# Issuing the normalising product of a projection unit two steps later, in a two-layer hybrid attention encoder

## The chip, the cores and the metric

The kernel runs on the 8 cores of one Trainium2 chip. Each core computes one of the 8 sequences of the batch, with the same program and its own data; the cores don't talk to each other. The metric is the device time in microseconds (us) of the slowest core.

## The reference

Two layers, each over 2048 tokens of width 1024 (per core):

```
h = rmsnorm(x)
q,k,v of 8 dilated heads | q,k,v of 8/2 grouped heads | two gates = split(h @ w_in)
q, k = rmsnorm per head (64 wide) of q and of k
branch A: three dilated windows per head, mixed by their softmax denominators
branch B: +-128 tokens, grouped queries, a sink logit per head
x += (sigmoid(ga) * (yA @ W_A) + sigmoid(gb) * (yB @ W_B)) @ W_out
x += SwiGLU(rmsnorm(x));   x += sigmoid(rmsnorm(x) @ W_pg) * (p @ W_pp)
```

What this text is about is the third line: every projected q and k of a head is multiplied by one over the root of its mean square and by a gain.

## The kernel before

The five engines run programs of their own and wait for each other by semaphores. A small recorder (class Sched) takes every operation in the order in which the Python code issues it, appends it to its engine's program, and adds the waits that the data need: a reader waits for the last writer, a writer for the last writer and all readers. So the order of issue in Python is the order on each engine, and an engine whose next instruction waits does nothing behind it. In the profile nearly all instructions therefore have one of two lines, L113 (with a semaphore update) and L116 (without).

All activations lie with the feature on the partition and the token on the free axis, in chunks of 512 tokens (n = 0 to 3). hT is the normalised input of the layer, ring the streamed weights, P (in the buffer YP) the softmax numerators, psb the 8 banks of PSUM, scr four buffers of 128x512.

A projection unit (qk_unit) makes 128 features (two heads) of q or k for one chunk: 8 matmuls of 128x512 into one bank, a Square on ScalarE (sq), and then its end part, fin: one matmul with a block of ones (ps<-sq,cst_b) into a second bank, so that each row holds the sum of squares of its head; on ScalarE the logarithm and the exponential (scr<-ps, scr<-scr); and on VectorE one product, "in PSUM bank times gain times scr" (scalar_tensor_tensor). A q product writes its target in the buffer X directly; a k product writes kst, and two DMAs on SyncE's queue carry the halves on. There are 52 such units a layer, 104 in all. The product is the last reader of the unit's bank. v units (v_unit, 16 matmuls of 256 columns; vb_unit, 32 of 128) have one copy in place of all that. weave puts the end part of a unit behind the fifth matmul (ninth, seventeenth for v) of the next unit.

Eight units a layer run before attention (upfront), the other 44 are woven into it. run_steps goes through the attention steps: 160 for branch A (4 pairs of heads, 40 steps each), then 92 for branch B. In step i it issues

- on TensorE the scores (up to 4 matmuls into one of two banks), on ScalarE their exp into P, and in each odd step on VectorE one multiplication of the last two P by the exponentiated bias (YP<-YP,Ebuf);
- a late operation, if one is due: the logarithm and exponential of the softmax denominators, and six steps after a group's end the two multiplications that finish the rows of yaT (YP<-X,G);
- from the queue of fill work as many matmuls as the step's share in credit allows (Fill.run; a 512-column matmul costs 0.216);
- on TensorE the values product of step i-4 into one of two output banks, and at a group's end its copy or addition into the accumulator on VectorE (X<-ps, X<-ps,X). In the first eight steps of a pair each step is a group of its own.

Woven units take their main bank in rotation from 4, 5, 6 and the sum-of-squares bank is always 7. The unit three places on thus writes the same main bank again, and its first matmul waits for the product. At the start of a pair (pre) the fill queue is drained, and the first scores of the new pair read all four chunks of q and k that were projected during the last pair.

In the code before, fin issues the product at once:

```
S.op("act", ... scr[ri], in_=psb[b2], func=AF.Ln ...)
S.op("act", ... scr[ri], in_=scr[ri], func=AF.Exp, scale=-0.5)
S.op("dve", ... out=out, in0=psb[bk], scalar=gain, in1=scr[ri] ...)
```

Of the kernel before, what the change touches and what calls it, by code (L numbers as in the profile page):

```python
# [185 lines left out]
def build(n_layers=2):  # L186
# [26 lines left out]
    with ExitStack() as stack:  # L213
# [83 lines left out]
        bank_ctr = [0]  # L297

        def bank8():
            b = bank_ctr[0] % 8  # L300
            bank_ctr[0] += 1
            return b

        ctr = {}

        def rot(name, opts):
            i = ctr.get(name, 0)
            ctr[name] = i + 1
            return opts[i % len(opts)]
# [92 lines left out]
        def wdone(key):  # L402
            wissue(slot_of.pop(key))


        class Fill:
# [10 lines left out]
            def run(self, budget):  # L417
                self.credit += budget
                while self.q and self.credit >= self.q[0][0] * 0.5:
                    c, fn = self.q.popleft()  # L420
                    self.credit -= c
                    fn()
                if not self.q:
                    self.credit = 0.0

            def drain(self):
                while self.q:
                    self.q.popleft()[1]()
                self.credit = 0.0
# [13 lines left out]
        def norm_b(l, gcol, n, pair=True):  # L443
            bk = bank8()
            c0 = 4 if pair else 0
            for c in range(c0, NCH):
                S.op("pe", lambda e, c=c: e.matmul(psb[bk][:, :], lhsT=ones_b, rhs=hc(c, n), start=(c == c0), stop=(c == NCH - 1)),
                     reads=[("h", c, n), "cst_b"], writes=[("ps", bk)], inc=(c == NCH - 1))
            ri = rot("scr", range(4))
            S.op("act", lambda e: e.activation(out=scr[ri][:, :], in_=psb[bk][:, :], func=AF.Ln, bias=1024.0 * EPS),  # L450
                 reads=[("ps", bk)], writes=[("scr", ri)])
            S.op("act", lambda e: e.activation(out=scr[ri][:, :], in_=scr[ri][:, :], func=AF.Exp, scale=-0.5),
                 reads=[("scr", ri)], writes=[("scr", ri)])
            for c in range(NCH):
                S.op("dve", lambda e, c=c: e.scalar_tensor_tensor(
                    out=hc(c, n), in0=xc(c, n), scalar=vd[:, l * NVL + gcol + c:l * NVL + gcol + c + 1], in1=scr[ri][:, :],
                    op0=ALU.mult, op1=ALU.mult),
                    reads=[("x", c, n), ("scr", ri)] + VD, writes=[("h", c, n)])


        def qk_unit(l, key, wcol, width, n, gcol, dst, banks, stat, split=None):
# [18 lines left out]
            def fin():  # L480
# [3 lines left out]
                     reads=[("sq", si), "cst_b"], writes=[("ps", b2)])  # L484
                ri = rot("scr", range(4))
                S.op("act", lambda e: e.activation(out=scr[ri][:, :], in_=psb[b2][:, :], func=AF.Ln, bias=64.0 * EPS),
                     reads=[("ps", b2)], writes=[("scr", ri)])
                S.op("act", lambda e: e.activation(out=scr[ri][:, :], in_=scr[ri][:, :], func=AF.Exp, scale=-0.5),
                     reads=[("scr", ri)], writes=[("scr", ri)])
                if split:  # L490
                    ki = rot("kst", range(4))
                    dst_ = [(ALLP, kst[ki][:, :], False, [], [("kst", ki)])]
                else:
                    dst_ = dst
                for rows, out, tr, rk, wk in dst_:
                    i0, i1 = psb[bk][rows, :], scr[ri][rows, :]
                    if tr:
                        i0 = i0.rearrange("p (s r) -> p r s", r=16)
                        i1 = i1.rearrange("p (s r) -> p r s", r=16)
                    S.op("dve", lambda e, i0=i0, i1=i1, out=out, rows=rows: e.scalar_tensor_tensor(  # L500
                        out=out, in0=i0, scalar=vd[rows, l * NVL + gcol:l * NVL + gcol + 1], in1=i1, op0=ALU.mult, op1=ALU.mult),
                        reads=[("ps", bk), ("scr", ri)] + rk + VD, writes=wk)
                if split:
                    outs, wk = split(n)
                    for rows, out in outs:
                        S.dma("sp", lambda e, rows=rows, out=out: e.dma_start(out=out, in_=kst[ki][rows, :]), ("kstc", ki),
                              reads=[("kst", ki)], writes=wk)
            return [(0.216, mm(k)) for k in range(8)], (0.216, fin)
# [124 lines left out]
        def late_flush():  # L633
            while late:
                late.popleft()[1]()
# [3 lines left out]
        def run_steps(steps, fill, look):  # L639
            n = len(steps)  # L640
            slots = {}
            for i in range(n + look):
                if i < n:
# [15 lines left out]
                    if i % 2 == 1:  # L659
# [6 lines left out]
                             reads=[("P", ps - 1), ("P", ps), ("E", st["e"])], writes=[("P", ps - 1), ("P", ps)])  # L666
                    now[0] = i
                    if late and late[0][0] <= i:
                        late.popleft()[1]()
                    fill.run(st["fill"])  # L670
                if i >= look:
# [16 lines left out]
                    if st["last"]:  # L688
                        g["post"](ob_)
            late_flush()  # L690

        def e_rep(h, off, width, rep):
# [201 lines left out]
        def merge_units(l, h, banks, x_half=None):  # L894
            out = []
            for m in range(8):
                for n2 in range(2):
# [3 lines left out]
                    def mm(which, k, m=m, n2=n2, n=n, st=st):  # L901
                        def f():
                            if x_half is not None and which == "Ga" and m < 4:
                                ri = rot("scr", range(4))
                                st["ra"] = ri
# [30 lines left out]
                            if which in ("Ga", "Gb"):  # L936
                                ri = rot("scr", range(4))
                                st["r" + which[1]] = ri
# [60 lines left out]
        def run_all(units):  # L999
            for _, f in units:  # L1000
                f()

        x_v = x_d.rearrange("(c p) t -> p c t", p=128)
# [82 lines left out]
        for l in range(n_layers):  # L1086
# [27 lines left out]
            if l == 0:  # L1114
# [19 lines left out]
                flips(3)  # L1134
                clear_kb(K_GS)
            wdone(("A", l, 0))
            vb0 = l * NVL
# [6 lines left out]
            for part in ("p3", 0, 1, 2, 3):  # L1144
                vt_loads(0, part)
            dbank = lambda: rot("dense", (4, 5, 6))
            sbank = lambda: 7
            kq = [kb_unit(l, n, dbank, sbank) for n in range(NTC)] + [vb_unit(l, t, dbank) for t in range(4)]
# [23 lines left out]
            for c in range(4):  # L1172
# [12 lines left out]
                def pre(c=c):  # L1185
                    fill.drain()
                    fill.add(segs[c])
                ps_[0]["pre"] = pre
# [8 lines left out]
            for n in range(2):  # L1197
                S.alias(R_X(n), K_X01[n])
                load_x(src_x, n, skey(n), (1,))
            mbank = lambda: rot("mbank", (4, 5, 6, 7))  # L1200
            rest = weave([qbu[(cc, n)] for n in (2, 3) for cc in range(4)]) + [(0.0, lambda l=l: wdone(("QB", l)))]
# [11 lines left out]
            def pre_of(b):  # L1213
                if b == 0:
                    fill.add(rest)
                if b == 8:
                    assert ("QB", l) not in slot_of
# [46 lines left out]
            def gu_half(fb, cb, w, mi, fi, half):  # L1264
# [14 lines left out]
                for n in ns:  # L1279
                    ri = rot("scr", range(4))  # L1280
                    bg, bu = bks[(0, n)], bks[(1, n)]
# [57 lines left out]
            def ple(n, ms):  # L1339
                for m2 in ms:  # L1340
# [9 lines left out]
                    for k in range(2):  # L1350
                        S.op("pe", lambda e, k=k, bP=bP, m2=m2: e.matmul(
                            psb[bP][:, :], lhsT=WPP[:, k, m2 * 128:(m2 + 1) * 128], rhs=ppT[:, k, n * TC:(n + 1) * TC], start=(k == 0), stop=(k == 1)),
                            reads=["wpp", "ppT"], writes=[("ps", bP)], inc=(k == 1))
                    ri = rot("scr", range(4))
                    S.op("act", lambda e, bG=bG, ri=ri: e.activation(out=scr[ri][:, :], in_=psb[bG][:, :], func=AF.Sigmoid),
# [113 lines left out]
```

How the kernel before makes its waits and increments, by code:

```python
    def _waits(self, eng, toks, rawkeys):  # L78
        need = {}
        for (k, v) in toks:
            if v > need.get(k, 0):
                need[k] = v
        for k, v in need.items():
            if k == eng and (eng == "pe" or k not in rawkeys):
                continue
            if self.waited[eng].get(k, 0) >= v:
                continue
            self.waited[eng][k] = v
            s = self._sem(k)
            self.prog[eng].append(lambda e, s=s, v=v: e.wait_ge(s, v))
            self.nwait += 1
# [8 lines left out]
    def op(self, eng, fn, reads=(), writes=(), inc=True):  # L100
        toks = self._deps(reads, writes)
        raw = set()
        for r in reads:
            st = self.res.get(r)
            if st and st[0]:
                raw.add(st[0][0])
        self._waits(eng, toks, raw)
        s = self._sem(eng)
        call = _capture(fn)
        if inc:
            self.count[eng] += 1
            tok = (eng, self.count[eng])
            self.prog[eng].append(lambda e, c=call, s=s: getattr(e, c[0])(*c[1], **c[2]).then_inc(s, 1))
        else:
            tok = (eng, self.count[eng] + 1)
            self.prog[eng].append(lambda e, c=call: getattr(e, c[0])(*c[1], **c[2]))
        self._record(tok, reads, writes)
# [1 line left out]
    def dma(self, eng, fn, chan, reads=(), writes=()):  # L119
# [4 lines left out]
        tok = (chan, self.count[chan])  # L124
        call = _capture(fn)
        self.prog[eng].append(lambda e, c=call, s=s: getattr(e, c[0])(*c[1], **c[2]).then_inc(s, 16))
        self._record(tok, reads, writes)
```

## Time and profile before

| | us |
|---|---|
| median of 3 runs | 2242.71 (2242.6 to 2243.81) |
| the profiled execution | 2242.86 |
| its span, slowest core (core 3) | 2241.3 |
| spans of the 8 cores | 2232.8 to 2241.3 |
| TensorE busy on core 3 | 2081.4 (93%) |
| VectorE busy | 1126.8 (50%) |
| ScalarE busy | 947.0 (42%) |

The span is the time from a core's first instruction to its last; the device time of the same execution is 1.6 us more. Shares over the whole span mix stages. Attention with its woven projections takes about 84 to 332 us and 1188 to 1436 us of the span (up to the end of the last woven projection); in these stretches ScalarE and VectorE are far busier than on average. Matmuls are pipelined: one of 512 columns is shown with 0.38 us but follows the one before it after 0.21 us. "Granted clock" is the TensorE clock that the chip let through, as a share of full speed; 1.00 is 2.4 GHz, 0.50 is 1.2 GHz, and a stretch between them holds some of each.

### The profile page before, as it was taken

Reading aid. Unit: us, or ns where it says so; the run is one execution under the profiler, and the core shown is the slowest. Engines: PE = TensorE matmul, PEld = TensorE weight load, DVE = VectorE, ACT = ScalarE, POOL = GpSimd, SP = SyncE. Lnnn points to the kernel's source line nnn. Section 1 sums busy time; section 2 is a strip of 40 time slices with the busy share of each in tenths; the row PEclk is TensorE's granted clock in tenths of the full one; section 3 lists DMA queues with packets and bytes.
Section 4 is the critical chain, followed back from the end, with each engine's and each line's share of the span. In section 5 each row is a group of like instructions: output and inputs, shape, how many; then the busy total and the mean of one; then the engine's idle time right before and its main releaser. Section 6 shows DMA issues by size and latency. Waiting matters only on the chain.

```text
span 2241.3 us, 32719 instructions; the slowest of 8 cores (2232.8 to 2241.3 us)
## 1 busy us (share of the span) xinstructions
PE 2081.4 (93%) x11296; PEld 1023.9 (46%) x11296; DVE 1126.8 (50%) x1647; ACT 947.0 (42%) x1527; POOL 186.7 (8%) x201
## 2 busy tenths in 40 slices
PE   5888879899999999999989887898999999999998
PEld 1555534344444444444446564343444444444443
DVE  3677877555421221125855787765654112211376
ACT  4688886544311001113656888854523110011232
POOL 4110000000110000000130100000000100010000
PEclk9999999999999999999999999999999999999999
DMA  8752432474644203531253524253535721062113
GB/s 230 134 69 48 74 57 45 69 132 57 94 57 62 38 1 47 71 39 29 83 127 86 67 56 80 32 94 57 113 49 83 96 34 26 1 89 29 30 34 135
DMA packets 240187, 154.43 MB, mean 69 GB/s; under 512 B 88795, under 2 KB 217979, under 8 KB 239995
## 3 DMA queue, kind: packets, MB, share of 16 engines
q0 software_dynamic: 152240, 85.01, 29.1%
q1 hardware_dynamic: 87788, 67.33, 10.3%
q8 instruction: 96, 1.57, 0.3%
q14 instruction: 63, 0.52, 0.1%
HBM read 211.07 MB, written 21.00 MB: 104 GB/s over the span
## 4 chain that ended last, share of the span: by engine, by line
PE 83%; ACT 7%; issue 4%; DVE 4%; DMA 2%; ACTq 0%; DVEq 0%; POOL 0%; SPq 0%; POOLq 0%
PE ps L116 67%; PE ps L113 15%; ACT YP L113 2%; DVE X L113 2%; ACT G L113 2%; ACT scr L113 2%; DMA ring<-w_in 1%; DVE YP L113 1%; DVE hT L113 1%; ACT sq L113 1%; ACT hT L113 0%; ACT L113 0%; DMA X<-kst 0%; DVE scr L113 0%; ACTq L90 0%
## 5 line engine op out<-in xcount | busy, mean ns | idle before, releaser
L116 PE MATMUL ps<-hT,ring 128*128 128x512 bf16 x4536 | 1116.9, 382 | 13.6 <-DMA ring<-w_in 8.1
L116 PEld LDWEIGHTS ps<-hT,ring 128*128 128x128 bf16 x4536 | 443.1, 99 | 509.1 <-issue 28.3
L113 ACT ACTIVATE scr<-ps 128x512 f32<-128x512 f32 x480 | 274.7, 596 | 894.4 <-PE ps L113 871.7
L113 ACT ACTIVATE YP<-ps 128x512 bf16<-128x512 f32 x504 | 291.6, 592 | 158.5 <-PE ps L113 148.9
L113 DVE TENSOR_TENSOR G<-ps,scr 128x512 bf16<-128x512 f32 x176 | 113.4, 686 | 465.3 <-PE ps L113 465.3
L116 PE MATMUL ps<-G,YP 128*128 128x512 bf16 x1280 | 297.2, 379 | 0.0
L113 DVE TENSOR_TENSOR X<-ps,X 128x512 f32<-128x512 f32 x192 | 131.1, 688 | 177.8 <-PE ps L113 177.6
L113 PE MATMUL ps<-hT,ring 128*128 128x512 bf16 x648 | 218.2, 381 | 0.1
L113 DVE TENSOR_TENSOR YP<-YP,Ebuf 128x1024 bf16<-128x1024 bf16 x252 | 173.1, 688 | 84.3 <-ACT YP L113 83.3
L116 PEld LDWEIGHTS ps<-G,YP 128*128 128x128 bf16 x1280 | 125.3, 98 | 151.0
L113 PE MATMUL ps<-YP,G 128*128 128x512 bf16 (+2 forms) x536 | 159.5, 301 | 6.3 <-DVE X L113 3.5
L113 DVE SCALAR_TENSOR_TENSOR hT<-X,vd,scr 128x512 bf16<-128x512 f32 x192 | 129.3, 746 | 60.7 <-ACT scr L113 60.7
L116 PE MATMUL ps<-YP,G 128*128 128x128 bf16 (+2 forms) x864 | 126.0, 243 | 34.3 <-DVE X L113 28.4
L113 DVE SCALAR_TENSOR_TENSOR scr<-scr,ps 128x512 f32<-128x512 f32 x128 | 86.4, 686 | 95.9 <-PE ps L113 91.9
L113 ACT ACTIVATE hT<-X 128x2048 bf16<-128x2048 f32 x48 | 89.9, 1901 | 91.7 <-DVE X L113 88.8
L116 PE MATMUL ps<-X 128*128 128x128 bf16 (+1 forms) x768 | 102.7, 230 | 23.8 <-ACT YP L113 17.5
L116 PEld LDWEIGHTS ps<-YP,G 128*128 128x128 bf16 x864 | 72.1, 99 | 104.9 <-issue 57.2
L116 PE MATMUL ps<-G,ring 128*128 128x512 bf16 x448 | 109.4, 379 | 6.7 <-DVE X L113 6.7
L126 POOL DMA_DIRECT2D ring<-w_in x66 | 58.1, 889 | 614.8 <-PE ps L113 558.1
L113 PE MATMUL ps<-X,G 128*128 128x512 bf16 x216 | 83.2, 385 | 16.3 <-ACT YP L113 15.7
L113 PEld LDWEIGHTS ps<-hT,ring 128*128 128x128 bf16 x648 | 63.8, 98 | 72.3 <-issue 2.1
L113 ACT ACT_TABLE_LOAD x46 | 59.0, 1283 | 84.7 <-PE ps L113 78.6
(82 smaller groups left out, 1813.6 us busy)
## 6 DMA issues: line engine op xcount, KB each, us to landing
ring<-w_in POOLq DMA_DIRECT2D x42, 512.0 KB, 8.1
X<-x SPq DMA_DIRECT2D x16, 1024.0 KB, 13.8
YP<-w_ffn_down POOLq DMA_DIRECT2D x8, 1408.0 KB, 18.5
ring<-w_ffn_gate POOLq DMA_DIRECT2D x20, 512.0 KB, 6.2
ring<-w_ffn_up POOLq DMA_DIRECT2D x20, 512.0 KB, 7.9
ring<-w_out POOLq DMA_DIRECT2D x8, 1024.0 KB, 9.6
xscr<-X SPq DMA_DIRECT2D x8, 1024.0 KB, 4.2
X<-xscr SPq DMA_DIRECT2D x8, 1024.0 KB, 8.6
```

Source lines behind the costliest of these rows:

```text
L113: self.prog[eng].append(lambda e, c=call, s=s: getattr(e, c[0])(*c[1], **c[2]).then_inc(s, 1))
L116: self.prog[eng].append(lambda e, c=call: getattr(e, c[0])(*c[1], **c[2]))
L126: self.prog[eng].append(lambda e, c=call, s=s: getattr(e, c[0])(*c[1], **c[2]).then_inc(s, 16))
```

## The change

The product, and the DMAs behind it, go into a function tail that is not called at once but held. A counter called clock is advanced by 0.44 at each attention step and by the listed cost of each piece of fill work (0.216 for a matmul of 512 columns). A held tail is issued when the counter has gone on by 2.6 since its fin. In branch A a step with its fill adds between 0.9 and 1.2 to the counter, so that 2.6 is two to three steps. Whoever takes a bank or a scr buffer that a held tail still reads (claim) has it and all older ones issued first, and all are issued at the start of a pair, at the end of a run of steps, before block 0 and block 8 of branch B, and after upfront.

```diff
+        clock = [0.0]
+        held = collections.deque()
+        def hold(delay, bank, si, fn):
+            held.append((clock[0] + delay, bank, si, fn))
+        def tick(c):
+            clock[0] += c
+            while held and held[0][0] <= clock[0]:
+                held.popleft()[3]()
+        def claim(bank=None, si=None):
+            while any((bank is not None and h[1] == bank) or (si is not None and h[2] == si) for h in held):
+                held.popleft()[3]()
+        def held_flush():
+            while held:
+                held.popleft()[3]()
...
@@ Fill.run, Fill.drain, run_all: after each piece of work
                     fn()
+                    tick(c)
...
@@ qk_unit, fin
-                ri = rot("scr", range(4))
+                ri = next_scr()
...
-                for rows, out, tr, rk, wk in dst_:
-                    ... product on VectorE ...
-                if split: ... two DMAs on SyncE's queue ...
+                def tail():
+                    for rows, out, tr, rk, wk in dst_:
+                        ... product on VectorE ...
+                    if split: ... two DMAs on SyncE's queue ...
+                hold(2.6, bk, ri, tail)
...
@@ run_steps
                     now[0] = i
+                    tick(0.44)
                     if late and late[0][0] <= i:
                         late.popleft()[1]()
...
             late_flush()
+            held_flush()
...
@@ start of a pair
                 def pre(c=c):
                     fill.drain()
+                    held_flush()
```

No operation is added or removed.

## Rows read from the trace of the kernel before

**Rows 1.** Spans and mean granted TensorE clock, fastest and slowest core.
```profile
core 1: 2232.8 us, clock 0.990
core 3: 2241.3 us, clock 0.985
```

**Rows 2.** Busy time by stretch, layer 0, branch A then start of B: stretch, length, engines, PEclk, DMA.
```profile
84.00:292.00 208.00, 176.57 (x1651) 121.34 (x1649) 157.77 (x219) 169.99 (x312) 15.92 (x16) 0.96 0.40 70
292.00:332.00 40.00, 31.69 (x138) 13.01 (x139) 28.07 (x41) 34.39 (x63) 3.97 (x6) 0.96 0.42 76
```

**Rows 3.** Waits, 84 to 332 us: who for whom, us in total, times, longest.
```profile
ACT YP L113 <- PE ps L113: 25.3, 41, 2.2
DVE X L113 <- ACT scr L113: 17.5, 16, 2.5
PE ps L116 <- DVE X L113: 14.2, 13, 3.5
DVE kst L113 <- ACT scr L113: 11.5, 10, 3.1
```

**Rows 4.** Timeline, pair 0: start, length, engine, operation, [idle before, releaser].
```profile
118.34 1.07 ACT L113 ACTIVATE YP<-ps 128x512 bf16<-128x512 f32 x2
118.35 0.81 PE L116 MATMUL ps<-hT,ring 128*128 128x512 bf16 x3
118.54 1.10 DVE L113 SCALAR_TENSOR_TENSOR X<-ps,vd,scr 128x512 bf16<-128x512 f32 x1 [0.93 <-ACT scr L113]
119.55 0.69 DVE L113 TENSOR_TENSOR YP<-YP,Ebuf 128x1024 bf16<-128x1024 bf16 x1
120.09 0.27 PE L116 MATMUL ps<-ring,hT 128*128 128x256 bf16 x1
120.15 2.42 DVE L113 TENSOR_TENSOR YP<-X,G 64x512 bf16<-64x512 f32 x2
120.44 0.58 ACT L113 ACTIVATE sq<-ps 128x512 bf16<-128x512 f32 x1
```

**Rows 5.** Timeline, the same pattern in pair 1, and its last case in layer 1.
```profile
172.21 2.40 DVE L113 TENSOR_TENSOR YP<-X,G 64x512 bf16<-64x512 f32 x2
172.34 0.59 PE L116 MATMUL ps<-hT,ring 128*128 128x512 bf16 x2
...
1329.85 2.39 DVE L113 TENSOR_TENSOR YP<-X,G 64x512 bf16<-64x512 f32 x2
1329.92 0.39 PE L116 MATMUL ps<-ring,hT 128*128 128x128 bf16 x4
```

**Rows 6.** Timeline, starts of pair 2 and pair 3.
```profile
189.50 0.53 PE L116 MATMUL ps<-X 128*128 128x128 bf16 x3
190.41 0.69 DVE L113 TENSOR_TENSOR YP<-YP,Ebuf 128x1024 bf16<-128x1024 bf16 x1 [0.84 <-ACT YP L113]
...
239.78 0.38 PE L116 MATMUL ps<-X 128*128 128x128 bf16 x3 [0.16 <-ACT YP L113]
...
241.41 0.69 DVE L113 TENSOR_TENSOR YP<-YP,Ebuf 128x1024 bf16<-128x1024 bf16 x1 [0.25 <-ACT YP L113]
```

**Rows 7.** Timeline, branch B.
```profile
320.25 1.47 DVE L113 TENSOR_TENSOR X<-X,G 64x512 bf16<-64x512 f32 x2
320.49 0.59 PE L116 MATMUL ps<-hT,ring 128*128 128x512 bf16 x2
```

**Rows 8.** Timeline, a place without late multiplications.
```profile
114.09 0.68 DVE L113 TENSOR_TENSOR YP<-YP,Ebuf 128x1024 bf16<-128x1024 bf16 x1
114.19 0.27 PE L116 MATMUL ps<-ring,hT 128*128 128x256 bf16 x1
```

**Rows 9.** Timeline, start of pair 1.
```profile
146.45 0.75 DVE L113 SCALAR_TENSOR_TENSOR kst<-ps,vd,scr 128x512 bf16<-128x512 f32 x1 [1.28 <-ACT scr L113]
147.95 0.33 PE L116 MATMUL ps<-YP,G 128*128 128x128 bf16 x3 [1.45 <-DVE X L113]
```

**Rows 10.** Busy time by stretch behind that wait, columns as in Rows 2.
```profile
152.00:156.00 4.00, 3.59 (x20) 1.90 (x21) 3.09 (x6) 1.20 (x2) 0.00 (x0) 0.68 0.14 35
```

More of the change, by code:

```diff
@@ L301, in bank8, with next_scr @@
             bank_ctr[0] += 1
+            claim(bank=b)
             return b
+        def next_scr():
+            ri = rot("scr", range(4))
+            claim(si=ri)
+            return ri
         ctr = {}
@@ L427, in drain @@
                 while self.q:
-                    self.q.popleft()[1]()
+                    c, fn = self.q.popleft()
+                    fn()
+                    tick(c)
                 self.credit = 0.0
@@ L484, in fin @@
                      reads=[("sq", si), "cst_b"], writes=[("ps", b2)])
-                ri = rot("scr", range(4))
+                ri = next_scr()
                 S.op("act", lambda e: e.activation(out=scr[ri][:, :], in_=psb[b2][:, :], func=AF.Ln, bias=64.0 * EPS),
@@ L489, in fin @@
                      reads=[("scr", ri)], writes=[("scr", ri)])
[L490 to L494, printed above, removed]
-                for rows, out, tr, rk, wk in dst_:
[L496 to L507, printed above, removed]
+                def tail():
+                    if split:
+                        ki = rot("kst", range(4))
+                        dst_ = [(ALLP, kst[ki][:, :], False, [], [("kst", ki)])]
+                    else:
+                        dst_ = dst
+                    for rows, out, tr, rk, wk in dst_:
+                        i0, i1 = psb[bk][rows, :], scr[ri][rows, :]
+                        if tr:
+                            i0 = i0.rearrange("p (s r) -> p r s", r=16)
+                            i1 = i1.rearrange("p (s r) -> p r s", r=16)
+                        S.op("dve", lambda e, i0=i0, i1=i1, out=out, rows=rows: e.scalar_tensor_tensor(
+                            out=out, in0=i0, scalar=vd[rows, l * NVL + gcol:l * NVL + gcol + 1], in1=i1, op0=ALU.mult, op1=ALU.mult),
+                            reads=[("ps", bk), ("scr", ri)] + rk + VD, writes=wk)
+                    if split:
+                        outs, wk = split(n)
+                        for rows, out in outs:
+                            S.dma("sp", lambda e, rows=rows, out=out: e.dma_start(out=out, in_=kst[ki][rows, :]), ("kstc", ki),
+                                  reads=[("kst", ki)], writes=wk)
@@ L903, in f @@
                             if x_half is not None and which == "Ga" and m < 4:
-                                ri = rot("scr", range(4))
+                                ri = next_scr()
                                 st["ra"] = ri
@@ L936, in f @@
                             if which in ("Ga", "Gb"):
-                                ri = rot("scr", range(4))
+                                ri = next_scr()
                                 st["r" + which[1]] = ri
@@ L999, in run_all @@
         def run_all(units):
-            for _, f in units:
+            for c, f in units:
                 f()
+                tick(c)
         x_v = x_d.rearrange("(c p) t -> p c t", p=128)
@@ L1145, in build, with dbank, sbank @@
                 vt_loads(0, part)
-            dbank = lambda: rot("dense", (4, 5, 6))
-            sbank = lambda: 7
+            def dbank():
+                b = rot("dense", (4, 5, 6))
+                claim(bank=b)
+                return b
+            def sbank():
+                claim(bank=7)
+                return 7
             kq = [kb_unit(l, n, dbank, sbank) for n in range(NTC)] + [vb_unit(l, t, dbank) for t in range(4)]
@@ L1186, in pre @@
                     fill.drain()
+                    held_flush()
                     fill.add(segs[c])
@@ L1199, in build, with mbank @@
                 load_x(src_x, n, skey(n), (1,))
-            mbank = lambda: rot("mbank", (4, 5, 6, 7))
+            def mbank():
+                b = rot("mbank", (4, 5, 6, 7))
+                claim(bank=b)
+                return b
             rest = weave([qbu[(cc, n)] for n in (2, 3) for cc in range(4)]) + [(0.0, lambda l=l: wdone(("QB", l)))]
@@ L1215, in pre_of @@
                     fill.add(rest)
+                if b in (0, 8):
+                    held_flush()
                 if b == 8:
@@ L1279, in gu_half @@
                 for n in ns:
-                    ri = rot("scr", range(4))
+                    ri = next_scr()
                     bg, bu = bks[(0, n)], bks[(1, n)]
@@ L1353, in ple @@
                             reads=["wpp", "ppT"], writes=[("ps", bP)], inc=(k == 1))
-                    ri = rot("scr", range(4))
+                    ri = next_scr()
                     S.op("act", lambda e, bG=bG, ri=ri: e.activation(out=scr[ri][:, :], in_=psb[bG][:, :], func=AF.Sigmoid),
```

## The prediction

> **What bounds the kernel now.** I read the page first. TensorE is busy for 93% of the span, but that is an average; the change touches only the units woven into attention, so the stretches that count are about 84 to 332 us and the same stretch of layer 1, 1188 to 1436. There I read the busy time by stretch, then the waits, and then the timeline of TensorE, VectorE and ScalarE around single products, beside the order in which the code issues them.
>
> The stretches show three engines that are all nearly full and none that is full: of 208 us TensorE 177, ScalarE 170, VectorE 158, and at the start of branch B ScalarE 34.4 of 40 [rows 2]. Such a stage is bound by its chain: scores, exp, multiplication by the bias, values product, and two score banks that let TensorE run only two steps ahead of the exps. The waits say what the change aims at: VectorE stands 17.5 + 11.5 = 29.0 us in layer 0 in front of a product that waits for the exponential (scr) of its unit, in 26 places, while TensorE waits 14.2 us for VectorE's output X [rows 3]. If the first caused the second, it would pay to move the products.
>
> The timeline says that mostly it doesn't. Take the product at 118.54, for which VectorE waits 0.93 us; the bias multiplication behind it starts at 119.55. But this one needs two exps that ScalarE runs from 118.34 to 119.41, *behind* the unit's own exponential, since ScalarE too works in order [rows 4]. Without the product it would start at 119.5 at best. The wait in front of a product is a hole that ScalarE's order leaves in VectorE's time, and the product sits in that hole. Taken out of it, it is done later, and nothing else is done much earlier.
>
> **What the change does, part by part.** 104 products and the DMAs of those that go by kst are issued later, with the same lengths. So the question is only who waits for them, and who waited behind them. I placed each in the order of issue by adding up 0.44 a step and the costs of the fill work, which is arithmetic on the code, and looked up which rows stand before and behind that place.
>
> *Bank reuse behind late multiplications (cost).* In the case above the counter has gone on by 2.6 when TensorE is in the group of three matmuls at 118.35. By then VectorE's program holds, ahead of the product, the bias multiplication and the two multiplications YP<-X,G of 2.42 us together. VectorE comes to the product after 119.5 + 0.6 + 2.4 = about 122.1 (I give it half a microsecond for starting without the product) and ends it 1.1 us later, at 123.2. TensorE wants the bank, for the first matmul of the unit three places on, at 120.09 [rows 4]: a stall of 3.1 us where there was none. In pair 1 the same order ends the two multiplications at 174.6, the product at 175.6 or slightly before, and the bank is wanted at 172.34: 3.2 us; the pattern's last case is at 1329.85 and 1329.92, where the end is 1332.2 + 1.1 less 0.6: 2.8 us [rows 5]. There are three a layer. 2 x (3.1 + 3.2 + 2.8) = 18.2 us. The product's own place is what the code says, so this is the surest term; bounds 14 and 20.
>
> *Start of a pair (cost).* The last q product of pairs 1 and 2 comes due in the last step before the new pair, behind that step's bias multiplication, and the new pair's first scores read it. TensorE is there at 189.50; the bias multiplication runs at 190.41 to 191.10, so the product ends at 192.1: 2.6 us. Into pair 3 TensorE is there at 239.78, the bias multiplication at 241.41 and the product ends at 243.1, less 0.7 because what stood behind the old product moves up: again 2.6 us [rows 6]. Four in two layers, 10.4 us, bounds 7 and 12. Into pair 1 the product is done in time, since the fill work of pair 0 ends earlier.
>
> *Branch B (cost).* One place a layer has two multiplications of 1.47 us together ahead of the product, which then ends at 321.7 + 0.6 = 322.3, against a bank wanted at 320.49 [rows 7]: 1.8 us, 3.6 in all. The last units of B are not delayed, as gate units claim their banks at once.
>
> *Small shifts (cost).* At some 22 other places the product slips by one or two short VectorE instructions. In the one with the largest shortfall the bias multiplication ends at 114.8 and the product of 1.1 us would end at 115.9, less some 0.6 for starting earlier, against a bank wanted at 114.19: 1.1 us by this reckoning [rows 8]. The others lie between nothing and that, and a TensorE that has just stood still for one bank is less far ahead at the next. Bounds 0 and 22 x 1.1 = 24 us; I take 0.3 each, 6.6 us, nearer the low end since the long stalls come among them.
>
> *Copies that move up (gain).* In the first eight steps of a pair each step ends with a copy that frees an output bank, and there a ready copy does stand behind a waiting product. VectorE waits 1.28 us for the product at 146.45, the copy comes behind it, and TensorE stands for 1.45 us until 147.95 [rows 9]. There are four places like it, one at the start of each of pairs 1 and 2 in both layers; at the mean wait in front of a kst product, 11.5 / 10 = 1.15 us [rows 3], that is 4.6 us gained, bounds 0 and twice that, 9.2, if the product's own length leaves the path too.
>
> *Elsewhere.* The eight units before attention have idle VectorE time around them and banks that are wanted microseconds later, so they cost nothing; the work that hides them is the v unit behind, and without it at most the 0.7 us of a copy, once a layer. In SyncE's queue the kst DMAs now stand behind at most two loads that were issued before; nobody needs their data before the next pair. Waits are neither added nor harder to meet.
>
> New stalls sum to 18.2 + 10.4 + 3.6 + 6.6 = 38.8 us. Not all of it lengthens the span, since ScalarE still has work while TensorE stands. In the first case ScalarE's work that was released before the stall ends at 121.02 [rows 4]. TensorE comes back at 123.2 and its next scores end about half a microsecond later, so ScalarE idles 2.6 us, of which 0.6 were idle before: 2.0 of 3.1 us. I take 0.6 of all, 23.3 us, bounds 0.4 and 0.8 (16 and 31). Less the gain of 4.6: +18.7 us on the profiled execution's 2242.86 (a span of 2241.3 and 1.6 around it), which is 2261.6. That execution is 0.15 us above the median of the runs, so 2261.4 for the median.
>
> By one rule of the Trainium skill the sum would be zero. Its page "Perfetto Trace Analysis", section "Identifying Performance Opportunities", has one improve the most-contended engine, the one with the highest occupancy, and look for what opens the gaps on it. VectorE is the least occupied of the three here [rows 2], so by that rule gaps moved about on it would change nothing, and the time would be 2242.9. The trace does not bear that out for this change, since its slack is at single banks and not in the mean.
>
> **The rivals.**
>
> *More low clock.* TensorE ran at its lower level, 1.2 GHz, for part of 152 to 156 us, behind the stalls at the start of pair 1 (0.68 granted over 4 us) [rows 10]. That is 0.32 x 4 x 2 = 2.6 us at half speed and 1.3 us of work lost, at least, since the stretch may go on. There are twelve new stalls of 1.8 to 3.2 us; if each brings one that is 16 us, if half of them do 8 us, for 2270 or more. For it: the slowest core has the lowest clock, and is 8.5 us behind the fastest [rows 1]. Against: cores of the same program differ in this, and the stalls that go away take some low stretches with them.
>
> The page "TensorE: Matmul & The Clock Gate", section "Part 1: The HAM clock gate", states that the lower clock is the default and that activity lifts it; by that rule new stalls can only add such stretches, which is this rival's time of 2270. The rows fit it where a low stretch follows a stall.
>
> *Absorbed.* ScalarE is the real limit, TensorE uses up the new stalls where it would have waited for exps anyway (ScalarE waited for TensorE for 25.3 us in 41 places [rows 3], so there is room both ways), and the small gain cancels the rest: 2244, within 2240 and 2247. Against it: in pair 0 the score matmuls hardly wait.
>
> *Faster.* The waits in front of the products are on the path after all. VectorE's multiplications and copies move up by what it waited, 29.0 us a layer [rows 3]; TensorE's stalls for VectorE's X, 14.2 us in layer 0 [rows 3] and about as much in layer 1, shrink by a third, 9.5 us, and no bank is wanted before its product. Its place is the first eight steps of a pair and its price 2242.9 - 9.5 = 2233. It decides if the new stalls for banks and first scores stay under some 7 us over both layers, that is, if VectorE runs ahead of my reckoning by the 2 us by which the products are late. I find it unlikely because of the multiplications YP<-X,G.
>
> That the change does nothing, because claims force the products out at once, can be excluded: by the sum of costs only 3 of 104 are issued by a claim.
>
> **How the numbers follow.** The sum as worked out (2251 to 2269): 0.48. With more low clock (2269 and above): 0.20. Absorbed: 0.17. Faster: 0.15. The predicted time is that of the first, 2261.4. The range takes it whole, reaches over most of the low-clock case to 2278, and down over part of the absorbed one to 2240; outside lie most of the faster case and a small part of the upper one. A change under 0.2% (4.5 us) can't be told from none here. Faster by more than that: 0.15; within: 0.17; slower: 0.48 + 0.20 = 0.68.
>
> **What would show it.** In the waits: VectorE's waits for ScalarE's scr nearly gone, from 29.0 us; in their place VectorE waits for the exps (ACT YP). TensorE's waits for VectorE's X up from 14.2 to 35 us or so in layer 0, with single ones near 3 us at a matmul ps<-hT,ring or ps<-ring,hT about 36 us after branch A's start, and one of 2 to 3 us at the first scores (ps<-X) of pairs 2 and 3. The wait of 1.45 us at the start of pair 1 shrinks below 0.5. The prediction is wrong if TensorE's waits for X grow by less than 7 us over both layers, or if they grow as said and the span does not: then the share of 0.6 was the error.

## The result, and the profile after

The change makes the kernel slower: two runs of 2310.76 and 2316.38 us against 2242.6 to 2243.8, a ratio of 1.0314, interval 1.0284 to 1.0345. Forecast were 2261.4, and 2278 as the upper end; the direction was right, the size was not. The profiled execution is the one of 2310.76. In some executions, the profiled ones of `e5_flush_before_pair` and `e12_half_repaired` among them, some cores ran at a lower clock than the rest; the times given below leave such executions out, the intervals of these two runs still hold some, and in these two I read core 3.

Spans and granted clock, fastest and slowest core of the changed kernel, against [rows 1]:

```profile
core 0: 2301.8 us, clock 0.978
core 7: 2309.2 us, clock 0.974
```

All eight cores are slower by about as much, and the clock is lower on each. Next comes the busy time by stretch of nearly the same work as in [rows 2]. Matmul for matmul, 332 us of the kernel before is 364.8 us here; the second window stops at 360, so that the two rows hold 12 matmuls fewer:

```profile
84.00:315.00 231.00, 182.35 (x1645) 124.35 (x1644) 156.05 (x216) 169.99 (x309) 15.15 (x16) 0.93 0.37 62
315.00:360.00 45.00, 30.67 (x132) 11.92 (x129) 29.10 (x42) 35.02 (x65) 3.97 (x6) 0.91 0.38 60
```

VectorE and ScalarE do the same work in the same busy time; TensorE is busy for 6 us more in the first stretch, at a clock of 0.93 instead of 0.96, and the rest is standing still. The waits of 84 to 360 us, against [rows 3]:

```profile
DVE YP L113 <- ACT YP L113: 80.5, 61, 4.5
ACT YP L113 <- PE ps L113: 47.9, 53, 3.0
PE ps L116 <- DVE X L113: 36.0, 19, 3.5
```

and, of the kernel before, 84 to 332 us:

```profile
DVE YP L113 <- ACT YP L113: 24.8, 32, 1.9
```

VectorE's waits for scr are gone, as the change intends. Its waits for the exps (ACT YP) grew by 55.7 us, by more than the 29.0 that went, as the exps themselves now wait longer for TensorE. TensorE's waits for VectorE's X went from 14.2 to 36.0 us, and to 40.1 if the window goes on to 365 us and so takes in the stall at 360.14; the forecast was "to 35". ScalarE now waits 47.9 us for TensorE instead of 25.3. Even the engine that was to be the limit starves.

Timeline of the first case of [rows 4] in the changed kernel:

```profile
120.01 0.69 DVE L113 TENSOR_TENSOR YP<-YP,Ebuf 128x1024 bf16<-128x1024 bf16 x1 [1.61 <-ACT YP L113]
120.62 2.37 DVE L113 TENSOR_TENSOR YP<-X,G 64x512 bf16<-64x512 f32 x2
123.03 1.06 DVE L113 SCALAR_TENSOR_TENSOR X<-ps,vd,scr 128x512 bf16<-128x512 f32 x1
124.24 0.27 PE L116 MATMUL ps<-ring,hT 128*128 128x256 bf16 x1 [2.57 <-DVE X L113]
```

The bias multiplication doesn't start earlier; it waits 1.61 us for exps where the product used to stand. The product comes behind 2.37 us of late multiplications, and TensorE starts 0.15 us after its end, having stood for 2.57 us. Two more places, the first scores of pair 2 and a gate unit of branch B:

```profile
201.11 1.06 DVE L113 SCALAR_TENSOR_TENSOR X<-ps,vd,scr 128x512 bf16<-128x512 f32 x1
202.42 0.52 PE L116 MATMUL ps<-X 128*128 128x128 bf16 x3 [3.02 <-DVE X L113]
...
357.14 0.69 DVE L113 TENSOR_TENSOR YP<-YP,Ebuf 128x1024 bf16<-128x1024 bf16 x1 [4.50 <-ACT YP L113]
357.75 1.47 DVE L113 TENSOR_TENSOR X<-X,G 64x512 bf16<-64x512 f32 x2
359.25 0.75 DVE L113 SCALAR_TENSOR_TENSOR X<-ps,vd,scr 128x512 bf16<-128x512 f32 x1
360.14 1.44 PE L116 MATMUL ps<-hT,ring 128*128 128x512 bf16 x3 [4.16 <-DVE X L113]
```

Since the order of TensorE's instructions is the same in both kernels, each matmul can be set beside itself. Three sums over both attention stretches come of that, and they carry the rest of this text:

- **single stalls**: what TensorE newly stands at the reader or the bank of a product, place by place: 65.3 us (38 banks with 48.8, six first scores with 16.5);
- **net stalls**: all of TensorE's stalls over 0.15 us, after minus before: +44.9 us, since other stalls shrink beside the new ones;
- **low clock**: the time at 1.2 GHz (0.50 granted), after minus before: +50.5 us.

The attention stretches are 66.4 us longer. The remainder, 66.4 - 44.9 = 21.5 us, I put down to matmuls running slower: 0.43 us for each us of low clock. That is a difference and not a measurement of its own; it also holds what changed in stalls under 0.15 us.

### The profile page after: what moved, and what is told of

Its sections match the earlier page's. It is cut to its first block, busy times and chain, and to the rows that moved or that the text cites. A ratio compares the mean times of both kernels' runs of the same rounds, so it can differ in the third digit from the quotient of the medians.

```text
span 2309.2 us, 32550 instructions; the slowest of 8 cores (2301.8 to 2309.2 us)
## 1 busy us (share of the span) xinstructions
PE 2104.4 (91%) x11296; PEld 1032.8 (45%) x11296; DVE 1127.3 (49%) x1647; ACT 951.2 (41%) x1527; POOL 186.6 (8%) x201
## 4 chain that ended last, share of the span: by engine, by line
PE 80%; ACT 7%; DVE 6%; issue 5%; DMA 2%; DVEq 0%; ACTq 0%; POOL 0%; SPq 0%; POOLq 0%
PE ps L116 66%; PE ps L113 15%; DVE X L113 3%; ACT YP L113 3%; DVE YP L113 2%; ACT G L113 2%; DMA ring<-w_in 1%; ACT scr L113 1%; DVE hT L113 1%; ACT sq L113 1%; ACT hT L113 0%; ACT L113 0%; DVE kst L113 0%; DMA X<-kst 0%; DVEq L90 0%
## 5 line engine op out<-in xcount | busy, mean ns | idle before, releaser
L116 PE MATMUL ps<-hT,ring 128*128 128x512 bf16 x4536 | 1128.5, 385 | 41.9 <-DVE X L113 26.9
L116 PEld LDWEIGHTS ps<-hT,ring 128*128 128x128 bf16 x4536 | 444.0, 99 | 549.2 <-issue 73.2
L116 PE MATMUL ps<-G,YP 128*128 128x512 bf16 x1280 | 297.2, 379 | 0.0
L116 PEld LDWEIGHTS ps<-G,YP 128*128 128x128 bf16 x1280 | 125.2, 98 | 151.0
L116 PE MATMUL ps<-YP,G 128*128 128x128 bf16 (+2 forms) x864 | 128.1, 246 | 23.9 <-DVE X L113 21.0
L116 PE MATMUL ps<-X 128*128 128x128 bf16 (+1 forms) x768 | 105.2, 235 | 36.6 <-DVE X L113 14.6
L116 PEld LDWEIGHTS ps<-YP,G 128*128 128x128 bf16 x864 | 75.2, 100 | 92.6 <-issue 44.6
L116 PE MATMUL ps<-G,ring 128*128 128x512 bf16 x448 | 109.7, 380 | 6.7 <-DVE X L113 6.7
L116 PE MATMUL ps<-ring,hT 128*128 128x256 bf16 (+1 forms) x728 | 89.9, 260 | 20.8 <-DVE X L113 17.5
```

The source lines that it names most:

```text
L116: self.prog[eng].append(lambda e, c=call: getattr(e, c[0])(*c[1], **c[2]))
```

## The experiments

My theory: the loss is TensorE standing at banks and first scores whose product is late, and the low clock that comes with it. The rivals: VectorE's new order or the later DMAs cost by themselves; ScalarE is the limit; the low clock has another reason.

**1. The late product without its bank** (`e1_late_no_bank`), and **2. the same on the kernel before** (`e2_early_no_bank`).

```diff
-  i0, i1 = psb[bk][rows, :], scr[ri][rows, :]
+  i0, i1 = scr[ri][rows, :], scr[ri][rows, :]
```

> The changed kernel, but the late product reads scr twice in place of its PSUM bank and scr, so that no bank is held by it (this leaves the projected value out of q and k). Order and number of instructions are those of the changed kernel; the product may be some tenths shorter. My theory: the added time is made by banks that come free late (some 49 us of single stalls at matmuls of the projection units, of which what the rest gives back is about 15) and the low clock behind them. Without them only the stalls at first scores of pairs (14.6 us) and part of the low clock are left: 2252 to 2265. Rival A, that VectorE's order itself, or late DMAs of k, costs the time: 2290 or more. Rival B, low clock that comes for another reason than stalls: 2260 to 2275 with a granted clock that stays below 0.980.

> The kernel before with the same edit (the product reads scr twice, not its bank), which leaves the projected value out of q and k. It tells what the bank costs when the product is early, and is the base for the run above. My theory: little, since most banks come free before they are wanted: 2236 to 2243. Rival: even the early products hold TensorE up, then 2225 or less.

Measured: 2262.3 to 2263.9 for the first (1.0089, 1.0073 to 1.0106), 2240.2 for the second (one run), 3 us under the kernel before. So holding the bank costs 2310.8 - 2263 = 48 us of the 68, or 45 if the 3 us are taken off, with the order on VectorE and the DMAs unchanged. Rival A (2290 or more) is out. Rival B is not: 2262 to 2264 us lies in its range as well as in that of my theory, five of the eight cores show a granted clock below 0.980, and beside only 15.2 us of single stalls there are 29.9 us more of low clock. Of the rest, 13.2 + 2.0 us are the six first scores, read in the timeline of core 5 of the first run. TensorE's waits for X over the whole span in this run, and then in the changed kernel (37.8 us in 30 places in the kernel before):

```profile
PE ps L116 <- DVE X L113: 43.0, 23, 3.5
```

```profile
PE ps L116 <- DVE X L113: 86.6, 44, 5.4
```

**3. Products ahead of the late multiplications** (`e4_ahead_of_late`), and **4. all of them issued four steps before a pair ends** (`e5_flush_before_pair`).

```diff
# 3, run_steps
-  late.popleft()[1]()
+  fn_ = late.popleft()[1]
+  if fn_ in heavy: held_flush()     # heavy: the operations YP<-X,G and X<-X,G
+  fn_()
# 4, each pair
+  ps_[36]["pre"] = held_flush
```

> The changed kernel, but held products are issued ahead of a late multiplication of branch A (YP<-X,G) or branch B (X<-X,G) whenever one comes due; all others stay two steps late. My theory: the stalls of 2.6 to 3.2 us at six banks and of 2.0 at two go (17.1 + 4.0 = 21 us), with the low clock that follows them (some 0.4 us for each us of stall): 2310.8 - 21 to 29 = 2282 to 2290. Rival, that only 0.6 of such stalls lengthens the span: 2298. Rival, that ScalarE sets the time: no change, 2308 or more.

> The changed kernel, but held products are issued at step 36 of each pair (four steps before its end), so that a product which the next pair's first scores read is late by less. My theory: the six stalls of 1.9 to 3.3 us at first scores (16.5 us) shrink to the 0.5 us of before or so: 2310.8 - 14 to 20 = 2291 to 2297. Rival, that these stalls are shared with ScalarE's work and cost only part: 2302 or more. If products that become due after step 36 are still late, the stalls stay and so does the time.

Measured: 2284.9 to 2285.4 for 3 (1.0189, 1.0168 to 1.0209), as expected; 2295.1 and 2295.6 for 4 (1.0271, 1.0212 to 1.033), as expected. The bank of the first case comes free 0.18 us late in place of 2.57, the first scores of pair 3 wait 0.39 us in place of 3.33. Both classes of stalls are real, and both cost more than their length: 25 us for 21 us of single stalls, 15.5 for 13.

**5. Nothing held in branch B** (`e6_no_hold_in_b`): `hold` is replaced by a direct call of the product there.

> The changed kernel, but the eight units woven into branch B issue their product at once, as before; in branch A all are held. My theory: the stalls at the banks of these units and of the gate units behind them go, in the changed kernel 0.49 + 2.00 + 4.16 + 1.53 us in layer 0 and 0.49 + 0.32 + 2.00 + (5.43 - 1.63) us in layer 1, 14.8 us in all, and the low clock behind them: by the ratios of the two runs before (25 us gained for 21 us of stalls, 15.5 for 11.3) that is 15 to 20 us, 2291 to 2296. Rival, that my claim in the prediction (gate units are not delayed) was right and these stalls belong to something else: 4 us, 2307.

Measured: 2298.7 to 2299.7 (1.0247, 1.0232 to 1.0262), 12 us less than the changed kernel. The 14.8 us of single stalls are gone, so the rival (4 us) is out, but the gain is under the 15 to 20 that I expected: where the product no longer holds TensorE up, the Square of the last unit does, as before. From core 3 of this run, and from the changed kernel, where that wait had shrunk:

```profile
351.90 0.38 PE L113 MATMUL ps<-sq,cst_b 128*128 128x512 bf16 x1 [3.00 <-ACT sq L113]
```

```profile
354.69 0.44 PE L113 MATMUL ps<-sq,cst_b 128*128 128x512 bf16 x1 [2.03 <-ACT sq L113]
```

**6. The three repairs together** (`e9_repaired`: 3, 4 and 5).

> The changed kernel with the three repairs together: held products ahead of late multiplications, all issued at step 36 of a pair, none held in branch B. My theory: what is left are the small shifts of branch A, by the single stalls of the two runs before about 20 us at banks and 3 to 5 us at first scores, and they cost their own length: 2243 + 24 = 2267, within 2260 and 2272. Rival, that the wait in front of early products is worth something, which shows once the large stalls are gone: 2250 or less. Rival, that the repairs add up without any rest: 2243.

Measured: 2258.2 to 2260.0 (1.0067, 1.0053 to 1.0082), 2 us below the range of my theory. 22.8 us of single stalls are left, none over 1.3 us, and the kernel is 16 us above the one before. This is the part of the loss that no repair at the large places reaches: products that slip by one or two short VectorE operations at 31 banks and four first scores. The first case of [rows 4] here:

```profile
122.11 1.08 DVE L113 SCALAR_TENSOR_TENSOR X<-ps,vd,scr 128x512 bf16<-128x512 f32 x1
123.10 2.42 DVE L113 TENSOR_TENSOR YP<-X,G 64x512 bf16<-64x512 f32 x2
123.33 0.27 PE L116 MATMUL ps<-ring,hT 128*128 128x256 bf16 x1 [0.18 <-DVE X L113]
```

**7. Half the delay** (`e7_delay_half`: `hold(1.3, ...)`), and **8. half the delay with the repairs** (`e12_half_repaired`).

> The changed kernel with a hold of 1.3 on the counter in place of 2.6, that is one to two steps. My theory, that each product costs what it is later than its bank or reader is wanted: about half of the products no longer pass the late multiplications and are one bias multiplication (0.69 us) less late, so that the single stalls fall from 63 to some 25 to 35 us and the time to 2265 to 2280. Rival, that the delay as such costs (products behind any bias multiplication): 2295 or more. Rival, that a short hold already takes the products out of VectorE's way at no cost: 2243 or less.

> The changed kernel with the short hold of 1.3 and the three repairs (ahead of late multiplications, issued at step 36 of a pair, none held in branch B). In the run with the short hold alone 10.3 us of single stalls were left and it took 2257.8, that is 14 us above the kernel before; four of them, 2 x 2.93 at the banks behind YP<-X,G and 2.5 + 0.5 in branch B, are what the repairs aim at. My theory: a late product costs by its stalls and the low clock behind them alone, so without them nothing is left of the loss, and the gain from copies that move up stays: 2238 to 2245. Rival, that moving products costs by itself: 2250 or more. Rival, that the waits in front of the products were on the path: 2233 or less, as the run in which no product waits.

Measured: 2257.1 to 2259.8 for 7 (1.006, 1.0047 to 1.0074), below the range that I had given, because far fewer banks come late than I thought: 10.3 us of single stalls are left, most of it in three (2.93 at the bank behind YP<-X,G in each layer, 2.5 at the last gate bank). Run 8 takes these away, 3.0 us remain, and the time is 2244.9 to 2247.1 beside 2243.6 to 2248.9 for the kernel before on that chip (0.9968, 0.9923 to 1.0013: no difference), at the upper end of my theory's 2238 to 2245 and above it. So in time, moving a product costs nothing where its bank isn't wanted; it also brings nothing. On core 3 of run 7 attention is 11.6 us longer, of which 5.1 are net stalls and the other 6.5 go with 20.3 us more of low clock. The stretch around the stall of 2.93 us in run 7, core 3:

```profile
120.00:124.00 4.00, 1.13 (x12) 0.52 (x9) 3.86 (x5) 1.87 (x4) 0.00 (x0) 1.00 0.02 4
124.00:128.00 4.00, 3.94 (x24) 2.87 (x25) 1.72 (x3) 1.17 (x2) 0.00 (x0) 0.57 0.26 64
128.00:132.00 4.00, 4.00 (x41) 2.94 (x40) 2.52 (x4) 3.82 (x8) 0.00 (x0) 1.00 0.15 35
```

TensorE stands, and right behind the stall the granted clock is 0.57 over 4 us, that is 3.4 us at 0.50, then 1.00 again. In the kernel before the same work ran at 1.00.

**9. What the change could gain at best** (`e3_early_no_wait`): the early product takes the normaliser of the unit before.

```diff
+  rj = (ri - 1) % 4
-  i0, i1 = psb[bk][rows, :], scr[ri][rows, :]
+  i0, i1 = psb[bk][rows, :], scr[rj][rows, :]
```

> The kernel before, but the product multiplies by the normaliser of the unit before (which is long there) in place of its own, so that VectorE never waits for the logarithm and exponential. The product stands at its early place (q and k are scaled by another token chunk's or head's normaliser). This is what the change could gain at best. My theory: the waits of 29 us a layer in front of products lie beside ScalarE's work; free of them only the copies and banks behind them move up: 2233 to 2241. Rival, that these waits are on the path: 2225 or less.

Measured: 2232.1 to 2242.4 (0.9963, 0.9949 to 0.9977), three of the five within 2232.1 and 2233.2: 8 to 10 us, at the lower edge of my range. Of the 58 us that VectorE waited in front of products in both layers, most comes back; VectorE waits for the exps in their place, 129.2 us in this run against 83.3 before (whole span):

```profile
DVE YP L113 <- ACT YP L113: 129.2, 144, 2.9
```

```profile
DVE YP L113 <- ACT YP L113: 83.3, 101, 4.1
```

Part of these 10 us also has nothing to do with the place of the product in attention: the upfront k units end earlier without their wait, and TensorE's wait for them (DMA X<-kst) falls from 5.7 to 1.2 us.

**10. The last end parts spaced** (`e8_space_last_end`), on the kernel before, for what its trace showed beside the change; **11. k products only past the copy of the same step** (`e10_past_copy`), on the kernel before; and **12. both** (`e11_past_copy_spaced`).

```diff
# 10, weave, last unit of the runs in pair 2, pair 3 and branch B
-                out.append(pend)
+                out += [(0.6, lambda: None)] * space + [pend]      # space = 2
# 11, k products of the first twelve steps of a pair
+  if defer[0] and split: held.append(tail)      # else: tail()
...
                     if st["last"]:
                         g["post"](ob_)          # the copy
+                held_flush()
```

> The kernel before, early products, with one other edit: the end part of the last unit of three of the woven runs a layer (pair 2, pair 3, branch B) is taken 1.2 of credit, about one or two steps, after its last matmul and not right behind it. In the trace of before TensorE stands there for the Square of the same unit, 2.2 to 3.0 us at three places in each layer, some 15 us in all. My theory: the stalls shrink to a fraction, and cost what stalls cost in the runs before, about their length: 2228 to 2234. Rival, that ScalarE's queue is what holds both, so the wait returns at the scores behind: 2240 to 2244. Other side: the last unit's product is later and its bank with it: 2246.

> The kernel before, but a k product that comes up in the first twelve steps of a pair is issued after the copy of the same step, so that it passes this copy and nothing else. This is the one gain my prediction saw in the change (a ready copy behind a waiting product, 4 x 1.15 = 4.6 us, bounds 0 and 9.2). Expected: 2236 to 2241. Rival, that it is absorbed behind ScalarE: 2243. Other side: a k product later by a copy (0.4 to 0.7 us) makes a bank late at two or more places a layer: 2245.

> The kernel of the run above together with the spaced last end parts that gave 2239.5 (0.9983 of before). If the two gains add: 2234 to 2237, faster than either kernel of the case. Rival, that both take the same wait (both touch the start of a pair): 2239.

Run 10 gives 2237.9 to 2243.0 (0.9983, 0.9973 to 0.9993), less than the 9 to 15 us that I expected. The same matmul before and in run 10:

```profile
186.26 0.38 PE L113 MATMUL ps<-sq,cst_b 128*128 128x512 bf16 x1 [2.33 <-ACT sq L113]
```

```profile
185.53 0.38 PE L113 MATMUL ps<-sq,cst_b 128*128 128x512 bf16 x1 [0.75 <-ACT sq L113]
```

And the stretches behind it (columns as in [rows 2]), before and in run 10:

```profile
188.00:192.00 4.00, 3.31 (x22) 2.48 (x23) 2.64 (x4) 3.27 (x7) 0.00 (x0) 0.50 0.13 33
```

```profile
189.00:193.00 4.00, 4.00 (x38) 2.62 (x36) 3.12 (x5) 3.60 (x8) 0.00 (x0) 1.00 0.25 60
```

Here the stall shrinks to a third and the low stretch behind it is gone. Over all, net stalls fell by only 1.8 us: over the whole span TensorE's waits for the Square (sq) fall from 27.1 to 17.2 us, but those for exps rise by 4.0 and those for VectorE's YP by 3.2; what is gained on core 3 is the clock, 17.8 us less at 1.2 GHz. Core 3 had more low clock than most cores before; by the mean clock of all cores (table below) it is some 5 us.

Run 11 gives 0.9993 (0.9982 to 1.0004), no gain, though what it was to do it does: TensorE's waits for X over the whole span fall from 37.8 us in 30 places to 32.2 in 20. On core 3 net stalls fell by 6.3 us and the low clock grew by 10.7, which at 0.43 is 4.6 us. The gain in waits was spent on the clock; why the clock fell there I can't say.

Run 12 gives 2233.5 to 2237.4 (0.9959, 0.9946 to 0.9973), 0.4% faster than the kernel before, and faster than both kernels of the case, as expected if the two gains add. It has none of the change's hold of two to three steps.

Single stalls, net stalls, low clock and time of the runs, all against the kernel before, in us. The last column is the mean granted clock over the cores of the executions counted (the kernel before: 0.987); 0.001 of it is 4.5 us of low clock over the span:

| run | single stalls | net stalls | low clock | attention longer by | time | clock |
|---|---|---|---|---|---|---|
| changed kernel | 65.3 | +44.9 | +50.5 | +66.4 | +68 | 0.975 |
| 5, none in B | 49.7 | +34.7 | +39.9 | +53.0 | +56 | 0.977 |
| 4, before a pair ends | 51.9 | +33.6 | +32.5 | +48.6 | +52 | 0.979 |
| 3, ahead of late | 44.0 | +29.3 | +17.2 | +36.8 | +42 | 0.980 |
| 6, repaired | 22.8 | +12.9 | +4.9 | +15.5 | +16 | 0.986 |
| 1, no bank | 15.2 | +4.6 | +29.9 | +16.1 | +20 | 0.979 |
| 7, half delay | 10.3 | +5.1 | +20.3 | +11.6 | +14 | 0.981 |
| 8, half, repaired | 3.0 | -5.6 | +1.7 | -5.0 | 0 | 0.983 |
| 9, no wait | 0 | -8.5 | +7.4 | -6.4 | -8 | 0.984 |
| 11, past copy | 0 | -6.3 | +10.7 | -3.0 | -2 | 0.984 |
| 10, spaced | 0 | -1.8 | -17.8 | -9.6 | -4 | 0.988 |
| 12, both | 0 | -5.9 | -12.3 | -11.8 | -9 | 0.987 |

(The columns from single stalls to attention are of one core each: core 7 of the changed kernel, core 5 of run 1, else core 3, against core 3 of the kernel before.) In each row "attention longer by" is net stalls + 0.3 to 0.55 times low clock. The runs with few but long stalls, 1 and 7, have the most low clock for what they stand; run 6, with only short ones, has hardly any.

The last column sets a limit to my theory. Runs 8, 9 and 11 have 6 to 9 us fewer net stalls than the kernel before, and still 13 to 18 us more low clock over the span by their mean clocks. (Core 3 of run 8, with its +1.7, is the fastest core of its execution and no fair sample.) So the stalls are shown as the cause of the larger part of the loss, since the time goes down when they are taken away. That the low clock comes from them is not shown: it is real in the changed kernel, 0.975 against 0.987, but the amount of standing alone doesn't decide it.

## Why the prediction was right in its direction and wrong in its size

*The reason against the change* held. VectorE's wait was a hole of ScalarE's order; taken away entirely (run 9) it brings 8 to 10 us, as the waits turn into waits for exps, and a delayed product is paid where its bank or reader is wanted first: at 38 banks and six first scores, for 104 products. What failed is the sum: places put at nothing, a share of 0.6 that was too low, and the low clock left out.

*Bank reuse behind late multiplications*: forecast 18.2, measured 2.57 + 3.19 + 2.77 + 2.58 + 3.20 + 2.76 = 17.1. Right, place by place.

*Start of a pair*: forecast 10.4 for pairs 2 and 3, measured 3.02 + 3.33 + 3.03 + 3.33 = 12.7. "Into pair 1 the product is done in time" was wrong: it comes due behind four VectorE operations of 0.7 us each (two bias multiplications, a copy, an addition) and the first scores wait 1.85 and 1.94 us. I had looked at when the fill work ends and not at what had been issued on VectorE since.

*Branch B*: forecast 3.6, measured 4.0 at the two places named. "The last units of B are not delayed, as gate units claim their banks at once" was the worst step: 4.16 + 1.53 us in layer 0, 5.43 against 1.63 in layer 1, 9.5 us. A claim issues the held product in the very moment in which the next user's matmul is issued; two of the three claimed products were claimed for just that bank, and they are the two longest stalls of the kernel. A claim makes the order right. It doesn't make it early. Small shifts of B add 1.3.

*Small shifts*: forecast 6.6 (22 x 0.3), measured 16.9 in 24 places of branch A, 0.7 each, within the bounds of 0 and 24 that I had given. My reason for the low end, that a TensorE which has just stood is less far ahead, doesn't hold: in run 6, with the long stalls gone, the small shifts at 24 banks of branch A come to the same 16.9 us.

Together 65.3 us where I had 38.8.

*The share of 0.6 and the gain of 4.6* made 18.7 of 38.8, that is 0.48. Net stalls over single stalls are 44.9 / 65.3 = 0.69, gains included.

*The low clock* was left out of the sum and made a rival with 0.20. It is no alternative to the other terms but comes on top of them: 50.5 us x 0.43 = 21.5 us. What brings it is open. I had put it at 8 to 16 by twelve stalls of 1.3 us each, nearer than my sum.

The error of 68.0 - 18.7 = 49.3 us is thus: missed stalls 26.5 x 0.69 = 18.3; the share on those I had, 38.8 x (0.69 - 0.48) = 8.1; low clock 21.5; outside attention 1.5.

*The waits for X* came out close to the forecast (36.0 or 40.1 us for 35), but in part by luck: the single stalls of this layer are 34.0 us where I had 19.4. Of these, 3.0 us are waits for kst products, which have a row of their own (PE ps L116 <- DVE kst), the last 1.5 to 5.7 lie behind the window, and old waits shrank by 3.5.

*Copies that move up* were seen rightly as waits and wrongly as time: the wait of 1.45 us of [rows 9] is gone in the changed kernel, and run 11 takes such waits away and gains nothing that clears the noise, as its low clock grows. The 4.6 us of gain in my sum did not come.

The absorbed and the faster rival fell with runs 1, 3 and 4. "Faster" would have been decided if the new stalls stayed under 7 us; run 8 is the kernel where they do (3.0), and it is level with the one before, not at 2233.

The Trainium skill, page "Perfetto Trace Analysis", section "Identifying Performance Opportunities", has one optimize the engine with the highest occupancy first. Read as my prediction read it, that moves on the least occupied engine are free, it gives 2242.9; the measured 2310.8 is against that reading. The same page, section "Optimizing Tensor Performance", has matmul groups rotate through different PSUM banks so that the evacuation of one overlaps the matmuls of the next; by run 1 that overlap is what the change lost, 45 to 48 us. The trace agrees. The page "TensorE: Matmul & The Clock Gate", section "Part 1: The HAM clock gate", has activity lift the clock from the lower level. The table agrees for the changed kernel and runs 3 to 6, where more standing came with more of the lower level; it does not for runs 8, 9 and 11, which have less standing and more of it.

## What to carry to other kernels

Before delaying a reader, list for each instance the bank or buffer it holds, who wants it next, when, and what will stand in front of the reader at its new place on its own engine; the mean load of that engine says nothing about it. A long stall of TensorE costs about its own length, and often more: taken away, the long stalls gave back 1.2 us of time per us in runs 3 and 4 and 0.8 in run 5; runs 1 and 7, left with few but mostly long ones, lie 1.3 to 1.4 us per us above the kernel before, and run 6, with none over 1.3 us, 0.7. Look at the granted clock of all cores and not of one before you put a cost down to it. A wait on an engine that has another wait right behind it is worth what remains when it is taken away entirely, and one run with other data in its place measures that before any scheduling is written.

## What the runs showed of the hardware beyond what was expected

Of two stalls alike, one can be followed by a low stretch of the clock and the other not. After the stall of 3.33 us at the first scores of pair 3 (layer 0, changed kernel) the clock is low, while after the one of 3.19 us at 182.78 it isn't:

```profile
262.00:266.00 4.00, 2.74 (x15) 1.86 (x16) 1.61 (x3) 0.92 (x2) 0.00 (x0) 0.59 1.20 153
266.00:270.00 4.00, 3.98 (x40) 2.58 (x37) 3.48 (x4) 2.95 (x6) 0.87 (x1) 0.98 1.13 162
```

```profile
184.00:188.00 4.00, 4.00 (x38) 2.60 (x35) 1.74 (x3) 3.37 (x7) 0.00 (x0) 1.00 0.29 69
```

By these rows the low stretch is 3.4 us long. As an estimate, by 0.43 us for each us of low clock, the same kind of stall costs 3.2 us at one place and 3.3 + 3.4 x 0.43 = 4.8 at the other. The cores of one run, with the same program, show mean clocks from 0.972 to 0.978 and spans 7.4 us apart. What decides whether a low stretch follows is open.
